# Page numbers read ahead of waits, window rows loaded behind the first value compress, half of the next second sequence's keys loaded ahead of the value pages

## What is computed

```python
def history(pool, new):
    return concatenate([pool[page_table].reshape(b, past, KV, DH), new])
kcc = compress(history(pool_ck, kc), pe[0], w1[0], w2[0])   # "cmp_k" pages
vcc = compress(history(pool_cv, vc), pe[1], w1[1], w2[1])   # "cmp_v" pages
o_cmp, p = cmp_attention(q, kcc, vcc, pos)
idx, ok = select_blocks(p, pos, n_slc)                      # 16 of 33 blocks
o_slc = selected_attention(q, k_sel, v_sel, pos, kpos, ok)  # "slc_k", "slc_v" pages
o_win = window_attention(q, win_k + kw, win_v + vw, ...)    # last 512 rows
# returned too: the window rows, moved on by the 4 new tokens
```

## Time and profile before

| | us |
|---|---|
| median of three executions | 1961.66 |
| lowest and highest | 1958.75, 1962.72 |
| the profiled execution's own time | 1962.13 |
| span of the trace in it | 1960.5 |
| busy in the span: TensorE, VectorE, ScalarE, GpSimd | 1798.1, 980.2, 691.0, 366.1 |
| first pair, from and to | 1119 to 1205 |
| second pair | 1205 to 1292.9 |
| third pair | 1292.9 to 1378.3 |
| fourth pair | 1378.3 to 1463.4 |

### The profile page before, as it was taken

How to read it: one execution, slowest core, us unless ns; L and a number is a source line. 1 busy time by engine, 2 the same in 40 slices (tenths; PEclk the granted TensorE clock), 3 DMA queues, 4 the chain that set the end, 5 groups by cost and what they waited for, 6 DMA issues and landing times.

```text
span 1960.5 us, 34957 instructions
## 1 busy us (share of the span) xinstructions
PE 1798.1 (92%) x13070; PEld 1611.5 (82%) x13070; DVE 980.2 (50%) x1456; ACT 691.0 (35%) x1209; POOL 366.1 (19%) x580
## 2 busy tenths in 40 slices
PE   8999787999999997997888899898979799999996
PEld 8999667999999997996555567565649799999996
DVE  3353287444443435225777664636544644444434
ACT  3222223333332223214666645444432433333222
POOL 0003514000000221010000164453523200000121
PEclk9999679999999998996998899999989899999998
DMA  6221121222223222240000087878742122222331
GB/s 269 86 70 62 38 76 48 97 86 88 93 85 86 88 92 97 86 162 16 1 1 1 19 263 228 274 234 269 231 158 84 58 87 90 90 86 85 89 89 46
DMA packets 89324, 206.17 MB, mean 105 GB/s; under 512 B 13289, under 2 KB 50698, under 8 KB 88466
## 3 DMA queue, kind: packets, MB, share of 16 engines
q1 hardware_dynamic: 71426, 145.00, 23.0%
q0 software_dynamic: 16800, 54.76, 8.5%
q10 hardware_dynamic: 1008, 5.16, 0.6%
HBM read 188.10 MB, written 16.76 MB: 104 GB/s over the span
## 4 chain that ended last, share of the span: by engine, by line
PE 82%; DVE 8%; issue 3%; ACT 2%; DMA 2%; SPq 1%; POOL 1%; POOLq 0%; DVEq 0%; ACTq 0%
PE ps L1311 60%; PE ps L679 3%; PE ps L680 3%; PE ps L609 2%; PE ps L623 2%; PE ps L791 2%; PE ps L599 2%; PE ps L730 1%; PE ps L682 1%; PE ps L683 1%; SPq L471 1%; DVE slots L1906 1%; DMA slots<-in_slc_v 1%; DMA slots<-in_slc_k 1%; PE ps L1356 1%
## 5 line engine op out<-in xcount | busy, mean ns | idle before, releaser
L1311 PE MATMUL ps<-x_parts,piece_parts 128*128 128x272 f32 x6528 | 836.8, 291 | 43.3 <-DVE x_parts L1910 35.1
L1311 PEld LDWEIGHTS ps<-x_parts,piece_parts 128*128 128x128 f32 x6528 | 829.3, 191 | 48.7 <-issue 26.0
L1699 DVE TENSOR_TENSOR piece_parts<-ring,piece_parts 128x1024 fp32r<-128x1024 f32 (+1 forms) x200 | 243.7, 1218 | 625.6 <-ACT piece_parts L1530 625.6
L1530 ACT ACTIVATE piece_parts<-ring 128x1024 fp32r<-128x1024 f32 (+1 forms) x200 | 208.6, 1043 | 583.7 <-PE ps L1311 562.6
L1311 PE MATMUL ps<-big_parts,piece_parts 128*128 128x272 f32 x2176 | 337.0, 291 | 10.4 <-DVE big_parts L1179 6.4
L1311 PEld LDWEIGHTS ps<-big_parts,piece_parts 128*128 128x128 f32 x2176 | 299.8, 191 | 11.7 <-issue 6.6
L1311 PE MATMUL ps<-hidden_parts,piece_parts 128*128 128x272 f32 x704 | 145.2, 288 | 0.0
L893 ACT ACTIVATE chunk_hi<-slots 128x512 fp32r<-128x512 f32 x128 | 78.8, 627 | 163.3 <-PE ps L682 163.2
L1065 DVE TENSOR_TENSOR slots_low<-slots,chunk_hi 128x512 fp32r<-128x512 f32 x128 | 86.2, 689 | 65.4 <-ACT chunk_hi L893 65.0
L1311 PEld LDWEIGHTS ps<-hidden_parts,piece_parts 128*128 128x128 f32 x704 | 110.6, 189 | 0.0
L2045 POOL COPY slots<-slots 128x2 f32 (+1 forms) x44 | 21.4, 487 | 463.0 <-ACT slots L1659 463.0
(11 more groups left out here) (312 smaller groups left out, 2006.5 us busy)
## 6 DMA issues: line engine op xcount, KB each, us to landing
ring<-in_w_up SPq DMA_DIRECT2D x88, 512.0 KB, 3.4
ring<-in_w_in SPq DMA_DIRECT2D x48, 512.0 KB, 3.4
ring<-in_w_down SPq DMA_DIRECT2D x32, 512.0 KB, 3.5
slots<-in_cmp_k SPq DMA_DIRECT2D x128, 128.0 KB, 2.6
slots<-in_cmp_v POOLq DMA_DIRECT2D x128, 128.0 KB, 2.5
slots<-in_slc_k SPq DMA_DIRECT2D x128, 128.0 KB, 5.4
slots<-in_slc_v POOLq DMA_DIRECT2D x96, 128.0 KB, 2.5
ring<-in_w_out SPq DMA_DIRECT2D x16, 512.0 KB, 3.5
```

The lines of the kernel that those rows point to most:

```text
L1311: mm = pe.matmul(ps[:, 2 * psum_set + h, 0:HT], split[:, slot % 2, w_part, k * 128:(k + 1) * 128], rhs(k)[v_part][:, h * HT:(h + 1) * HT], ...
L1530: act.activation(split[:, s % 2, 0, 0:size], raw[s][:, 0:size], ACT.Copy).then_inc(w_hi, 1)
L1699: ve.tensor_tensor(split[:, s % 2, 1, 0:size], raw[s][:, 0:size], as_f32(split[:, s % 2, 0, 0:size]), ALU.subtract).then_inc(w_lo, 1)
```

## The change

`load_pages` is taken apart: `page_numbers` reads the numbers, and `load_pages` takes them. On both queues the read now stands ahead of the wait. GpSimd waits for cv0 before it issues the window rows, and loads the first sequence's slc_v behind them. SyncE issues half of the next pair's cmp_k of slot 1 behind ss1, ahead of the wait for cv1, and the other half where all of it was.

```diff
--- before.py
+++ after.py
@@ -462,11 +462,15 @@
             sl = CHUNKS[name] // 8
             return v.rearrange("p (s n) -> p s n", s=4)[:, sl, :].rearrange("p (pg c n) -> p c pg n", pg=NPG, c=8)
 
-        def load_pages(eng, cache, slot, r, b, first=0, count=NPG, ahead=0, landed=None):
+        def page_numbers(eng, r, b, first=0, count=NPG, ahead=0):
 
             _, pages = nc.values_load_multi_w_load_instructions(ptab[0:1, bass.ds(r * 32 + (32 * ahead + b * NPG + first), count)],
                                                                engines=(eng.engine,), min_val=0, max_val=NPHYS - 1,
                                                                skip_runtime_bounds_check_because="a page table holds pages")
+            return pages
+
+        def load_pages(eng, cache, slot, pages, first=0, landed=None):
+
             for g, v in enumerate(pages):
                 eng.dma_start(slots[:, slot, (first + g) * 256:(first + g + 1) * 256],
                               A[cache][bass.ds(v, 1), :, :].rearrange("a p n -> (a p) n")).then_inc(landed or slot_in[slot], 16)
@@ -478,16 +482,24 @@
                 sp.wait_ge(XP.sem, XP.at(name, r))
                 sp.sem_inc(turn, 1)
 
+            half = NPG // 2
             for b in range(2):
+                pages = page_numbers(sp, r, b)
                 after(f"ck{b}")
-                load_pages(sp, "slc_k", b, r, b)
+                load_pages(sp, "slc_k", b, pages)
             if not last:
+                pages = page_numbers(sp, r, 0, ahead=1)
                 after("ss0")
-                load_pages(sp, "cmp_k", 0, r, 0, ahead=1)
+                load_pages(sp, "cmp_k", 0, pages)
+                pages = page_numbers(sp, r, 1, 0, half, ahead=1)
+                after("ss1")
+                load_pages(sp, "cmp_k", 1, pages)
+            pages = page_numbers(sp, r, 1, 0, half)
             after("cv1")
-            load_pages(sp, "slc_v", 3, r, 1, 0, NPG // 2, landed=half_in)
+            load_pages(sp, "slc_v", 3, pages, landed=half_in)
             if not last:
-                load_pages(sp, "cmp_k", 1, r, 1, ahead=1)
+                pages = page_numbers(sp, r, 1, half, half, ahead=1)
+                load_pages(sp, "cmp_k", 1, pages, half)
 
         def feed_in1(eng, part, take):
 
@@ -509,7 +521,7 @@
             sp.dma_start(ptab[:, :], A["page_table"]).then_inc(tab_in, 16)
             sp.wait_ge(tab_in, 16)
             for b in range(2):
-                load_pages(sp, "cmp_k", b, 0, b)
+                load_pages(sp, "cmp_k", b, page_numbers(sp, 0, b))
             with sp.Fori(0, 3) as r:
                 key_pages(sp, r, False)
             key_pages(sp, 3, True)
@@ -1204,6 +1216,7 @@
 
             def pair(r):
                 prev = not (isinstance(r, int) and r == 0)
+                pages = page_numbers(po, r, 0)
                 if prev:
                     po.wait_ge(XP.sem, XP.at("pv1", r - 1))
                     po.wait_ge(win_out, 128 * r)
@@ -1213,19 +1226,17 @@
                         c0 = g * 32 + h * 16
                         op = po.tensor_copy(qb[64 * h:64 * h + 64, :, g, c0:c0 + 16].rearrange("p b (j t) -> p b j t", j=4), src)
                 op.then_inc(XQ, 1)
-                for b in range(2):
-                    load_pages(po, "cmp_v", 2 + b, r, b)
+                load_pages(po, "cmp_v", 2, pages)
+                load_pages(po, "cmp_v", 3, page_numbers(po, r, 1))
+                pages = page_numbers(po, r, 0)
+                po.wait_ge(XP.sem, XP.at("cv0", r))
+                po.sem_inc(turn_v, 1)
                 for b in range(2):
                     po.dma_start(win_k[:, b, :, :], A["win_k"][bass.ds(r * 2 + b, 1), :, :, :].rearrange("a p g n -> (a p) g n")).then_inc(win_in, 16)
                     for q in range(2):
                         po.dma_start(big[:, 12 + 2 * b + q, 0:512].rearrange("p (t n) -> p t n", t=2),
                                      A["win_v"][bass.ds(r * 2 + b, 1), 2 * q:2 * q + 2, :, :].rearrange("a t p n -> p (a t) n")).then_inc(win_in, 16)
-                def selected(b):
-                    po.wait_ge(XP.sem, XP.at(f"cv{b}", r))
-                    po.sem_inc(turn_v, 1)
-                    load_pages(po, "slc_v", 2 + b, r, b, (0, NPG // 2)[b], (NPG, NPG // 2)[b])
-
-                selected(0)
+                load_pages(po, "slc_v", 2, pages)
                 po.wait_ge(win_in, 96 * (r + 1))
                 po.sem_inc(turn_v, 1)
                 for b in range(2):
@@ -1237,7 +1248,10 @@
                     po.dma_start(ov[:, 124:252, :].rearrange("a p n -> (a p) n"), wv[:, 0, 256:512]).then_inc(win_out, 16)
                     po.dma_start(ov[:, 252:508, :].rearrange("a (t p) n -> p (a t) n", t=2),
                                  wv[:, 1, :].rearrange("p (t n) -> p t n", t=2)).then_inc(win_out, 16)
-                selected(1)
+                pages = page_numbers(po, r, 1, NPG // 2, NPG // 2)
+                po.wait_ge(XP.sem, XP.at("cv1", r))
+                po.sem_inc(turn_v, 1)
+                load_pages(po, "slc_v", 3, pages, NPG // 2)
 
             pair(0)
             with po.Fori(1, 4) as r:
```

## The result

| | us |
|---|---|
| before, median of 13 executions on one chip | 1959.64 (1952.34 to 1965.61) |
| changed, median of 13 | 1952.92 (1950.48 to 1955.58) |
| ratio | 0.9969, 95% interval 0.9958 to 0.9981 |
| own time and span of the profiled execution, changed | 1950.48, 1948.9 |

The change makes the kernel 0.31% faster, about 6.1 us. A second comparison, of 12 executions with 17 of before, gave 0.9971 (0.9957 to 0.9984). The two profiled executions lie 11.6 us apart, more than the medians: that of before took 1962.13 us, 2.5 us above its median, and that of after is the fastest of its 13. Single traces show here where time goes; how much it is on the mean comes from the timed runs.

The account below looks back on a forecast made before the run. TensorE bounds the kernel, through its waits and the clock lost behind them. Window rows -2.3 us, reads and landing of the selected values -3.8: -6.1 against 1962.1, so 1956.0 us; range 1946 to 1969, likeliest 1951 to 1959 (chance 0.38).

Parts of the forecast that it names:

- part two: Page numbers read ahead of the waits on SyncE and GpSimd: 0.8 to 1.0 us gained at L791, nothing for other reads.
- Part one: Window rows leave the time of the selected keys: all four waits at L730 gone, VectorE late next, 2.3 us gained.
- the bound of 8.7: Most that moving the window rows could gain, in us, if TensorE's clock stays up at L743 in each pair.
- the 2.8 us that they had to spare: Window rows in place about 9 us after L711, wanted by L743 at 11.8 us, hidden by VectorE.
- Part three: 9.44 MB ahead of the selected values: landing 11.0 us after L754; with the reads, -3.8 us over the four pairs.
- the 340 GB/s for full engines: Estimated DMA rate from L711 to the selected values, at which 9.44 MB take 27.8 us.
- No backlog to speak of: Second rival, chance 0.17: at 354 GB/s values land 9.6 us after L754, no pair waits 1 us; -16.4 us, 1946.
- The backlog that takes all back: First rival, chance 0.24: at 330 GB/s the values land 12.0 us after L754; -0.2 us in all, 1962.
- the slower outcome: Third rival, chance 0.15: at 310 GB/s the values land 14.2 us after L754; +6.4 us, 1969.
- marks set for "right": No L730 key wait, four L743 waits of 2.5 to 3 us on VectorE, L791 11 us after L754, 10.5 last.
- sign of being wrong: L743 released by the window rows, L730 still late, or L791 more than 12.1 or less than 10 us after L754.
- The mark of 15.5 us per pair: Time from the head sum (L711) to the second value compress (L679), claimed to be 15.5 us in each pair.

Follow-up runs that it names:

- masked scores first: Changed kernel with VectorE's value copy and masked scores moved ahead of three operations that nobody waits for so soon; 0.9935 of the kernel before.
- 10 and 6: Changed kernel with the second sequence's value pages divided 10 on SyncE and 6 on GpSimd instead of 8 and 8; 0.9940 of the kernel before.

## Why the prediction came out right, and where it did not

The sum was right (-6.1 us forecast, -6.1 by the ratio), and its agreement is luck: what the reads give was priced too low, what the half of the keys costs was not priced by itself, and the two roughly cancel. Nor do the traces bear its size out. From L711 of the first pair to the end of the last product with the values it is 302.77 us before and 290.67 after (290.61 in the second trace of the changed kernel), twice the forecast. Part of the gap is the trace of before, 2.5 us above its median; part is that L723 of the first pair comes 1.0 and 3.2 us later in the two traces than L711 did. Single traces can't close it.

**The step that failed is in part two: "I count 0.8 to 1.0 us there and nothing for the other reads, which stand before transfers with slack".** The reads alone bring 8.0 us. At L730 the second sequence's key pages are the last thing TensorE waits for: there is no slack there, and in the last three pairs the read ahead of these sixteen pages lay on the path. With the reads ahead the waits in these pairs fell by 1.6, 1.5 and 1.7 us, more than the one read of 0.98 us; that GpSimd's value pages also start and end a read sooner is a likely part of it, which no run here separates. And from 2.5 and 2.7 us they fell to 1.0, where the clock stayed up. At L791 the read on the path was GpSimd's 0.56 us, not SyncE's 0.98, so there the forecast took too much.

**Part one: right in kind, the size open.** All four key waits are gone with the window move, VectorE took their place, and its waits of 2.66 to 2.94 us are the 2.9 forecast. But I took the first pair's 15.52 us for all; the clock did not fall each time, and the sum of the four pairs fell by 5.3 instead of 2.3 us in the first trace, inside the bound of 8.7, and by 1.6 in the second (15.54, 16.35, 15.61 and 15.28). There the second pair waited 3.87 us for the window rows: the 2.8 us that they had to spare are not there in each pair. What I missed is that the reads do the same work: moved alone the window rows bring 2.7 us, beside the reads nothing that shows, and, with overlapping intervals, 3.1 to 3.5 us when the half of the keys stands there too. The two gains (2.7 and 8.0) don't add, as they take away the same waits.

**Part three: the landing was off, and that the bytes set it is not shown.** The values were forecast 11.0, 11.0, 11.0 and 10.5 us behind L754; they came at 9.74, 10.64, 11.88 and 11.55. The step that is off is the 340 GB/s for full engines: behind the three microseconds of start they moved 364, 344 and 365 GB/s for 22.5 to 24 us. Over the whole stretch, start and hole included, it was 326, 314 and 327 GB/s. So 0.6 MB was left at the first compress' end and 1.1 MB at the second, of the 1.5 MB that the forecast had. In the last two pairs GpSimd's pause of 1.8 us ahead of its eighth page came on top, which stood in the trace of before and which I did not price; without it the third pair's values came at 10.37 us. And without the window stores, 2.1 MB less ahead of them, the first two pairs' values came no sooner (9.99 and 11.43 us). The half of the keys, to which the forecast gave no cost behind the values and 3 us of transfer ahead of them, costs 5.5 us without the window move and about 3.9 with it.

**The rivals.** No backlog to speak of (1946) is what the first pair's trace looks like, but not the others. The backlog that takes all back and the slower outcome did not come. The 436 GB/s of the Trainium skill (DMA: Bandwidth & Descriptors, Anatomy of one DMA — SWDGE (gpsimd) path) were not seen in the stretches of the changed kernel either: 344 to 365 GB/s with the engines full, 410 in the fastest four microseconds (1342 to 1346). Of the marks set for "right", no wait on slc_k was met in both traces of the changed kernel, and four waits on VectorE of 2.5 to 3 us in the first; the second had three and the one on the window rows, which the prediction had named a sign of being wrong. So was a landing less than 10 us behind L754 (9.74 in the first pair). The mark of 15.5 us per pair was not met.

## What to carry to other kernels

Price a register read or any other small step that stands between a wait and the transfers behind it by the wait that ends last on those transfers, not by its own engine's idle time; here reads of 0.98 us on the chain in three pairs and of 0.56 us in all four were worth 8.0 us, clock included, and moving 2.1 MB of window rows alone 2.7. Two edits that take away the same wait don't add, so time them apart: of this change's three parts one carries it, one brings nothing measurable beside the first alone, and one costs. Bytes moved ahead of an urgent transfer are not free because they were wanted later anyway. And an edit to one engine's instructions can move a pause that has nothing to do with what the edit was for: read the issue times of that engine in both traces before you put the gain down to the bytes.

## What the runs showed of the hardware

A wait's length did not decide on TensorE's clock. Before the product with the values, waits of up to 1.89 us in the changed kernel left it at 2.4 GHz (7.1 us of work). But with the window rows alone a wait of 1.64 us, and with reads and window rows one of 1.77, were followed by 8.81 us, while waits of 2.67 us (no window stores) and 2.35 us (masked scores first) were followed by 7.13 and 7.12. In the changed kernel's first trace waits of 2.94, 2.84, 2.84 and 2.66 us at L755 were followed by 3.60, 2.47, 1.94 and 3.21 us for the same eight matmuls, so that one ran wholly at 2.4 GHz, one almost wholly at 1.2 and two across a change of level. The stretches around the second pair's L755, columns as above with the granted clock ahead of the last two:

```profile
1250.00:1254.00 4.00, 1.16 (x14) 0.56 (x13) 3.71 (x9) 0.00 (x0) 4.00 (x8) 1.00 1.02 339
1254.00:1258.00 4.00, 4.00 (x20) 2.39 (x17) 3.96 (x3) 0.00 (x0) 3.63 (x8) 0.59 0.96 309
```

So the same program can lose more or less clock at the same place: in the changed kernel's second trace all four took 3.46 to 3.59 us. The kernel before ran from 1952.34 to 1965.61 us on one chip; how much of that spread is the clock no run here shows. In the 10 and 6 kernel the clock fell in the third pair with no wait over 0.6 us in the 17 us ahead (granted 0.70 from 1353 to 1356): the 16 matmuls with the window values took 3.28 us instead of 1.90.

```profile
1354.02 1.00 PE L790 MATMUL ps<-ring 127*64 127x256 f32 x4 [0.52 <-DVE ring L1144]
1354.80 3.28 PE L794 MATMUL ps<-big,ring 128*64 128x256 f32 x16
```

Ahead of them TensorE had waited 0.28, 0.41 and 0.52 us in short succession.

GpSimd's issues stop for 1.2 to 1.8 us at some places in the loop over the pairs, with nothing in the trace that releases them. In two traces of the changed kernel the long ones stand ahead of the same instructions (1.73 and 1.72 us in the loads of the second pair's pages, 1.78 and 1.78 us ahead of the third pair's eighth value page), and with fewer instructions ahead (10 and 6, no window stores) they stand elsewhere. The cause stays open.
